# The first half of each expert's gate and up weights as one 4 MB transfer with 32 KB to a partition, in place of two of 2 MB with 16 KB

## The chip, the cores and the metric

One Trainium2 chip, one of its cores. The metric is the time on the device in microseconds (us), for the program from start to end, of one execution. Several executions of the same kernel are timed and the median is given.

## What is computed

The reference is one layer of a decoder block: 512 tokens of width 1024, in float32. An RMS norm and one input projection feed two attention branches (sliding window with sinks, and forgetting attention), whose gated outputs are added to x. Then comes the part that this document is about, a mixture of 32 experts with the top 4 for each token:

```python
logits = t @ w_router + b_router                       # t: the tokens after the second RMS norm
top_val, top_idx = lax.top_k(logits, 4); gate = softmax(top_val)
...
gu = xb @ w_gate_up[e] + b_gate_up[e]                  # w_gate_up[e]: 1024 x 2048, 8 MB
g, u = gu[:, :1024], gu[:, 1024:]
g = minimum(g, 7.0); u = clip(u, -7.0, 7.0)
a = (u + 1.0) * (g * sigmoid(1.702 * g))
return a @ w_down[e] + b_down[e]                       # w_down[e]: 1024 x 1024, 4 MB
```

The results are weighted with the gates and added to x. All 32 experts' weights, 12 MB each, are read once or more from HBM.

## The kernel before, in words

The first 420 us are the attention part. It streams w_in, w_o and w_out through two staging buffers (loop over `g`, lines 511 to 527), and its end frees the memory that the experts' weights go into.

Then the experts are worked off one at a time. The work on one expert is an item i; items are ordered so that even ones have room for 96 tokens (three groups of 32) and odd ones for 64 (two groups). Item 0 is done ahead of the loop, a loop over `pair` does items 1 and 2, 3 and 4, and so on (15 pairs here), and item 31 comes last (lines 1921 to 1969). An expert with more tokens than its room gets further items; the trace here has 32.

**Weights.** The 8 MB of gate and up weights of an item have one place in SBUF: six of the eight chunks of 128 rows in `gu_head`, two in `gu_tail`. They are loaded in four transfers of 2 MB (`load_gu`, line 546), q = 0 to 3. Each brings 256 neighbouring rows of the matrix, two neighbouring rows to a partition, so 16 KB in one piece to each partition (`w_gu_v`, line 349). So chunk k of an item does not hold the rows 128k to 128k + 127, but every second row of a block of 256 (`every_second`, line 441), and the tokens' values have to be laid out in the same order. The 4 MB of down weights come in two transfers of 2 MB (`load_dn`), with four rows to a partition, and have two places, `dn_even` and `dn_odd0/1`.

**Transfers.** SyncE (SP) issues all weight transfers in one queue, in the order of its program (lines 590 to 598): for item i the four of gate and up, then the two of down. Ahead of each it waits until TensorE has used what is in the place: `gu_used[q]` for q = 0, 1, 2, which TensorE raises after step k = 1, 3, 5 of `gate_up`, `bank_done` for q = 3, raised at step 7, and `dn_used[j]` for the down weights. The loads for item i + 1 are thus issued while item i runs.

**TensorE.** In `gate_up` (line 1843) it goes through the eight chunks k, for each group of tokens and each of four column blocks one matmul (line 1853). At even k it waits for the transfer that brings chunks k and k + 1 (`gu_in[k // 2]`). In even items of the loop it adds in between, after k = 1, 3, 5 and 6, the sums that bring the results of earlier items back to their tokens (`pair_sums`, line 1819). After `gate_up(i)` come a few small matmuls for the next list of tokens (line 1799) and `down(i - 1)` (lines 1888 and 1896).

**Tokens.** POOL fetches the rows of the item's tokens from HBM with an indirect DMA (`xg`, line 693, on a queue of its own). VectorE turns them in blocks of 32x32 into `xT` (even items) or `xT_odd` (`turn_rows`, line 1284): for each group and each quarter of 32 partitions one transpose of 32x256, with the columns picked two neighbours to a partition (line 1295), then a multiplication with the norm's gains, `g2_near`, laid out in the same order (loaded at line 543). For item 0 TensorE picks the rows itself by matmuls with a selection matrix (`first_rows`, line 1804), whose stationary operand is read with a step of 2 (line 1809).

Of the kernel before, what the change touches and what calls it, by code (L numbers as in the profile page):

```python
# [28 lines left out]
P = 128  # L29
# [27 lines left out]
def hybrid_block(nc, x, positions, norm1_g, w_in, b_forget, b_gate, q_norm_swa, k_norm_swa, sinks,  # L57
# [41 lines left out]
    with ExitStack() as ctx:  # L99
# [230 lines left out]
        ps = ctx.enter_context(nc.psum_tensor("ps", [P, 8, 512], F32))  # L330
        SUM_STEPS = (1, 3, 5, 6)
        SUM_BANKS = slice(6, 8)
        LAST_BANKS = (slice(0, 2), slice(2, 4), slice(6, 8), slice(4, 6))
# [14 lines left out]
        w_out_v = w_out[0].rearrange("(k p) n -> p k n", p=P)  # L348
        w_gu_v = w_gate_up.rearrange("l e (q p a) n -> (l e) q p (a n)", p=P, a=2)
        w_dn_v = w_down.rearrange("l e (j p k) n -> (l e) j p (k n)", p=P, k=4)  # L350

# [7 lines left out]
        b_dn_in = sem("b_dn_in")  # L359
        gu_in = [sem(f"gu_in{q}") for q in range(KD // 2)]  # L360
        dn_in = [[sem(f"dn_in{a}{j}") for j in (0, 1)] for a in (0, 1)]
# [41 lines left out]
        xT_ps, xT_ready = sem("xT_ps"), sem("xT_ready")  # L403
        gu_used = [sem(f"gu_used{q}") for q in range(KD // 2)]
        bank_done, gu_out, gu_biased = sem("bank_done"), sem("gu_out"), sem("gu_biased")
# [34 lines left out]

        def every_second(t):
            return slice(t // 2 * 2 * P + t % 2, (t // 2 + 1) * 2 * P, 2)

# [62 lines left out]
        def _(sp):  # L506
# [4 lines left out]
            for g in range(G_END):  # L511
                if g >= 2:
                    sp.wait_ge(split_lo, g - 1)
                dst, s = st_w[:, g % 2], stage_in[g % 2]
                if g < 2 * N_WIDE:
                    c0 = g // 2 * 2 * GW
                    sp.dma_start(st_w_wide[g % 2], w_in_v[:, g % 2 * KH:(g % 2 + 1) * KH, c0:c0 + 2 * GW]).then_inc(s, 16)
                elif g < G_O:
                    c0 = g * GW if g < G_GATE else GATE + (g - G_GATE) * GW
                    sp.dma_start(dst, w_in_v[:, :, c0:c0 + GW]).then_inc(s, 16)  # L520
                elif g < G_OUT:
                    c0 = (g - G_O) * GW
                    sp.dma_start(dst[:, 0:4], w_oa_v[:, :, c0:c0 + GW]).then_inc(s, 16)
                    sp.dma_start(dst[:, 4:8], w_ob_v[:, :, c0:c0 + GW]).then_inc(s, 16)
                else:
                    c0 = (g - G_OUT) * GW
                    sp.dma_start(dst, w_out_v[:, :, c0:c0 + GW]).then_inc(s, 16)
                if g == 0:
                    sp.dma_start(wfl[:, :, 0:HF], w_in_v[:, :, FL:FL + HF]).then_inc(wfl_in, 16)
                if g == 1:  # L530
                    sp.dma_start(bf_bc[:, :], b_forget[0].partition_broadcast(P)).then_inc(small_in, 16)
                    sp.dma_start(sink_bc[:, :], sinks[0].partition_broadcast(P)).then_inc(small_in, 16)
                    sp.dma_start(brt[:, :], b_router[0].partition_broadcast(P)).then_inc(small_in, 16)
                    sp.dma_start(g_sw[:, 0, :], q_norm_swa[0].partition_broadcast(P)).then_inc(small_in, 16)
                    sp.dma_start(g_sw[:, 1, :], k_norm_swa[0].partition_broadcast(P)).then_inc(small_in, 16)
                    sp.dma_start(w_rt[:, :, :], w_router[0].rearrange("(k p) e -> p k e", p=P)).then_inc(small_in, 16)
                    with nc.allow_non_contiguous_dma(reason="a few hundred words onto partitions"):
                        sp.dma_start(pos_i[:, :], positions[0].rearrange("(c p) -> p c", p=P)).then_inc(small_in, 16)
                        for a, w in enumerate((q_norm_fox, k_norm_fox)):
                            for half in (0, 1):  # L540
                                sp.dma_start(g_fx[half * HD:(half + 1) * HD, a:a + 1],
                                             w[0].rearrange("(d o) -> d o", o=1)).then_inc(small_in, 16)
                        sp.dma_start(g2_near[:, :].rearrange("p (q a) -> p q a", a=2),
                                     norm2_g[0].rearrange("(q p a) -> p q a", p=P, a=2)).then_inc(small_in, 16)

            def load_gu(e, q):
                src = w_gu_v[e, q] if isinstance(e, int) else w_gu_v[bass.ds(e, 1), q].rearrange("a p n -> (a p) n")
                two = gu_head[:, 2 * q:2 * q + 2, :] if q < 3 else gu_tail[:, :, :]
                sp.dma_start(two.rearrange("p a n -> p (a n)"), src).then_inc(gu_in[q], 16)

# [5 lines left out]
            sp.wait_ge(m_sum, KD)  # L556
            for q in range(3):
                load_gu(0, q)
# [4 lines left out]
            sp.wait_ge(split_lo, G_END)  # L563
            load_gu(0, 3)

# [12 lines left out]
            def gu_free(q, i, pair=None):  # L578

                if q < KD // 2 - 1:  # L580
                    sp.wait_ge(gu_used[q], counted(2, i, pair))
                else:
                    sp.wait_ge(bank_done, counted(5, groups_before(i), pair))

            for q in range(KD // 2):
                gu_free(q, 1)
                load_gu(e1, q)
            sp.wait_ge(items_ready, 1)
            n_pairs = sp.value_load(pairs[0:1, 0:1], min_val=PAIRS, max_val=MAX_PAIRS)
            with sp.Fori(0, n_pairs) as pair:  # L590
                for i in (2, 3):
                    e = sp.value_load(experts[0:1, bass.ds(pair * 2 + i, 1)], min_val=0, max_val=E - 1)
                    for q in range(KD // 2):
                        gu_free(q, i, pair)
# [346 lines left out]
        def _(dve):  # L941
# [57 lines left out]
            v.memset(ekey_col[0:1, :], 65536.0)  # L999
            dve.wait_ge(small_in, 16 * 12)  # L1000
            then(v.tensor_copy(pos_f[:, :], pos_i[:, :]))
# [282 lines left out]
            def turn_rows(i, pair=None):  # L1284
# [3 lines left out]
                if i > 1:  # L1288
                    dve.wait_ge(bank_done, counted(5, groups_before(i - 1), pair))
                near = xg[:, :].rearrange("s (k p a) -> s p k a", p=P, a=2)  # L1290
                for n in range(groups(i)):
                    s = slice(n * GROUP, (n + 1) * GROUP)
                    for q in range(4):
                        r = slice(q * GROUP, (q + 1) * GROUP)
                        ins = v.transpose(turned_rows[r, :, s].rearrange("r (k a) s -> r k a s", a=2),  # L1295
                                          near[s, r].rearrange("s p k a -> s k a p"))
# [181 lines left out]
        def _(pe):  # L1478
# [323 lines left out]
            def first_rows(ks):  # L1802
# [3 lines left out]
                for k in ks:  # L1806
                    dst = xT_a[:, k, :] if k < 5 else xT_b[:, k - 5, :]
                    for c in range(NB):
                        ins = pe.matmul(dst, h2n[:, c, every_second(k)], sel_f[:, c, :], start=(c == 0), stop=(c == NB - 1))
                return ins  # L1810
# [32 lines left out]
            def gate_up(i, pair=None, last=False):  # L1843
# [4 lines left out]
                for k in range(KD):  # L1848
                    if k % 2 == 0:
                        pe.wait_ge(gu_in[k // 2], counted(32, i * 16 + 16, pair))  # L1850
                    for n in range(groups(i)):
# [3 lines left out]
                        if k == KD - 1:  # L1855
                            ins.then_inc(bank_done, 1)
                    if k % 2 and k < KD - 1:
                        ins.then_inc(gu_used[k // 2], 1)
                    if i == 2 and k in SUM_STEPS:
# [133 lines left out]
```

## Time and profile before

| | us |
|---|---|
| Median of 3 runs | 1430.1 |
| Lowest and highest | 1428.09 and 1431.43 |
| The profiled execution's own time | 1430.49 |
| Its span in the profile | 1428.7 |
| TensorE busy with matmuls | 1367.9 (96%) |
| VectorE busy | 747.2 (52%) |
| DMA | 447.28 MB, 313 GB/s in the mean over the span |

The profile is that of one execution. The span goes from the first to the last recorded instruction; the time on the device holds 1.8 us more. A busy TensorE in this table includes matmuls that overlap in its pipeline. The times in the rows below count from the start of the span. A transfer's "time to landing" goes from its issue on SP to the arrival of the last part of its data and so includes the wait behind the transfers that are still in the queue.

### The profile page before, as it was taken

Reading aid. Unit: us, or ns where it says so; the run is one execution under the profiler, and the core shown is the slowest. Engines: PE = TensorE matmul, PEld = TensorE weight load, DVE = VectorE, ACT = ScalarE, POOL = GpSimd, SP = SyncE. Lnnn points to the kernel's source line nnn. Section 1 sums busy time; section 2 is a strip of 40 time slices with the busy share of each in tenths; the row PEclk is TensorE's granted clock in tenths of the full one; section 3 lists DMA queues with packets and bytes.
Section 4 is the critical chain, followed back from the end, with each engine's and each line's share of the span. In section 5 each row is a group of like instructions: output and inputs, shape, how many; then the busy total and the mean of one; then the engine's idle time right before and its main releaser. Section 6 shows DMA issues by size and latency. Waiting matters only on the chain.

```text
span 1428.7 us, 27526 instructions
## 1 busy us (share of the span) xinstructions
PE 1367.9 (96%) x11224; PEld 648.9 (45%) x11227; DVE 747.2 (52%) x1486; ACT 223.1 (16%) x416; POOL 190.5 (13%) x242
## 2 busy tenths in 40 slices
PE   6999999999989999999999999999999999999998
PEld 5888887778953333323232322323232232323233
DVE  5213736755257475545645544564654446465544
ACT  4224436642220000000000000000000000000000
POOL 2001400000002112020211202021120202112020
PEclk9999999999999999999999999999999999999999
DMA  6232320003679999999999999999999999999993
GB/s 192 89 118 64 113 89 1 2 31 114 255 295 356 409 400 417 391 412 414 413 413 405 417 403 407 417 409 414 411 416 393 414 417 409 412 414 415 395 414 154
DMA packets 59704, 447.28 MB, mean 313 GB/s; under 512 B 8656, under 2 KB 26096, under 8 KB 35056
## 3 DMA queue, kind: packets, MB, share of 16 engines
q1 hardware_dynamic: 56480, 435.96, 76.5%
q0 software_dynamic: 3072, 10.49, 2.3%
q8 instruction: 28, 0.46, 0.1%
q10 hardware_dynamic: 112, 0.28, 0.1%
q14 instruction: 12, 0.10, 0.0%
HBM read 442.51 MB, written 4.19 MB: 313 GB/s over the span
## 4 chain that ended last, share of the span: by engine, by line
PE 74%; DMA 19%; issue 4%; DVE 2%; ACT 1%; POOL 0%; SPq 0%; DVEq 0%; POOLq 0%; ACTq 0%
PE ps L1853 31%; DMA gu_head<-in_w_gate_up_dram 10%; PE ps L1888 9%; DMA gu_tail<-in_w_gate_up_dram 9%; PE ps L1819 7%; PE ps L1512 3%; PE ps L1514 3%; PE ps L1513 3%; PE ps L1896 2%; PE ps L1536 2%; PE ps L1538 2%; PE ps L1537 2%; PE ps L1503 1%; PE ps L1505 1%; PE ps L1504 1%
## 5 line engine op out<-in xcount | busy, mean ns | idle before, releaser
L1853 PE MATMUL ps<-gu_head,xT 128*32 128x512 f32 x2304 | 257.1, 594 | 2.5 <-DMA gu_head<-in_w_gate_up_dram 2.4
L1343 DVE TENSOR_TENSOR x_tok<-x_tok,ps 128x1024 f32<-128x1024 f32 x64 | 77.9, 1220 | 249.4 <-PE ps L1819 249.4
L1853 PE MATMUL ps<-gu_head,xT_odd 128*32 128x512 f32 x1536 | 168.9, 593 | 0.7 <-DVE act_gu L1307 0.6
L914 ACT ACTIVATE act_s<-act_gu 128x768 f32<-128x768 f32 (+1 forms) x32 | 23.6, 738 | 925.3 <-DVE act_gu L1318 925.3
L1853 PEld LDWEIGHTS ps<-gu_head,xT 128*32 128x32 f32 x2304 | 70.8, 110 | 168.7 <-issue 158.0
L1307 DVE STREAM_TRANSPOSE act_gu<-ps 128x512 f32<-128x512 f32 x80 | 57.2, 715 | 142.1 <-PE ps L1853 137.1
L693 POOL DMA_INDIRECT xg<-h_dram,idx_g x32 | 69.9, 2186 | 441.8 <-DVE row_all L1276 441.8
L954 DVE TENSOR_TENSOR st_l<-st_w,st_h 128x2048 fp32r<-128x2048 f32 x25 | 57.3, 2292 | 113.7 <-ACT st_h L758 113.7
L1888 PE MATMUL ps<-dn_even,aT 128*32 128x512 f32 x1024 | 116.1, 594 | 0.0
L1888 PE MATMUL ps<-dn_odd,aT 128*32 128x512 f32 x960 | 106.1, 594 | 0.0
L1853 PEld LDWEIGHTS ps<-gu_head,xT_odd 128*32 128x32 f32 x1536 | 49.3, 110 | 116.5 <-issue 111.3
L1853 PE MATMUL ps<-gu_tail,xT_odd 128*32 128x512 f32 x512 | 68.1, 680 | 28.2 <-DMA gu_tail<-in_w_gate_up_dram 28.2
L1853 PE MATMUL ps<-gu_tail,xT 128*32 128x512 f32 x768 | 88.8, 596 | 0.0
L1295 DVE STREAM_TRANSPOSE xT<-xg 32x256 f32<-32x256 f32 x180 | 77.8, 432 | 2.3
L1888 PEld LDWEIGHTS ps<-dn_even,aT 128*32 128x32 f32 x1024 | 31.7, 110 | 68.0 <-issue 67.6
L1896 PE MATMUL ps<-dn_even,aT 128*32 128x512 f32 x512 | 60.8, 592 | 0.0
L1888 PEld LDWEIGHTS ps<-dn_odd,aT 128*32 128x32 f32 x960 | 29.7, 110 | 63.2 <-issue 62.8
L1295 DVE STREAM_TRANSPOSE xT_odd<-xg 32x256 f32<-32x256 f32 x128 | 55.2, 431 | 1.8 <-DMA xg<-h_dram,idx_g 0.2
L721 POOL COPY put_row<-row_all 128x1 f32 x15 | 2.8, 185 | 382.9 <-PE ps L1819 382.9
L1853 PEld LDWEIGHTS ps<-gu_tail,xT_odd 128*32 128x32 f32 x512 | 17.4, 122 | 77.8 <-DMA gu_tail<-in_w_gate_up_dram 39.4
L758 ACT CAST st_h<-st_w 128x2048 fp32r<-128x2048 f32 x25 | 47.6, 1905 | 32.1 <-PE ps L1538 30.1
L1512 PE MATMUL ps<-hT_h,st_h 128*128 128x512 f32 x128 | 50.0, 391 | 0.0
(389 smaller groups left out, 2030.8 us busy)
## 6 DMA issues: line engine op xcount, KB each, us to landing
gu_head<-in_w_gate_up_dram SPq DMA_DIRECT2D x96, 2048.0 KB, 23.7
gu_tail<-in_w_gate_up_dram SPq DMA_DIRECT2D x32, 2048.0 KB
dn_even<-in_w_down_dram SPq DMA_DIRECT2D x32, 2048.0 KB, 25.1
dn_odd<-in_w_down_dram SPq DMA_DIRECT2D x32, 2048.0 KB, 21.4
st_w<-in_w_in_dram SPq DMA_DIRECT2D x17, 1024.0 KB, 5.3
st_w<-in_w_out_dram SPq DMA_DIRECT2D x4, 1024.0 KB, 5.1
x_tok<-in_x_dram SPq DMA_DIRECT2D x4, 512.0 KB, 5.7
st_w<-in_w_o_swa_dram SPq DMA_DIRECT2D x4, 512.0 KB, 3.5
```

Source lines behind the costliest of these rows:

```text
L693: g.indirect_dma_start(out=xg[0:n, :], out_offset=None, in_=h2_dram[:, :], in_offset=bass.IndirectOffsetOnAxis(ap=idx_g[0:n, 0:1], axis=0) ...
L758: sc.copy(st_h[:, g % 2], st_w[:, g % 2]).then_inc(split_hi, 1)
L954: v.tensor_tensor(st_l[:, g % 2], st_w[:, g % 2], st_h[:, g % 2].bitcast(F32), ALU.subtract).then_inc(split_lo, 1)
L1295: ins = v.transpose(turned_rows[r, :, s].rearrange("r (k a) s -> r k a s", a=2), near[s, r].rearrange("s p k a -> s k a p"))
L1307: ins = v.transpose(act_gu[:, :, n * GROUP:(n + 1) * GROUP].rearrange("p (b k) s -> p b k s", k=4), ps[:, n, :].rearrange("p (b r k) -> p ...
L1343: v.tensor_tensor(x_tok[:, c, :].rearrange("p (h n) -> p h n", h=2), x_tok[:, c, :].rearrange("p (h n) -> p h n", h=2), ps[:, banks, :], A ...
L1512: pe.matmul(dst, wh[:, k], xh[:, k], start=(k == 0), stop=False)
L1513: pe.matmul(dst, wh[:, k], xl[:, k], start=False, stop=False)
L1819: ins = pe.matmul(ps[:, banks, :][:, h], table[rows, c * P:(c + 1) * P], half[rows, :], start=(at == 0 and half is y_hi[y]), stop=(at == l ...
L1853: ins = pe.matmul(ps[j * GROUP:(j + 1) * GROUP, n, :], rows_of(i)[:, k, n * GROUP:(n + 1) * GROUP], gu_columns(k, j), start=(k == 0), stop ...
L1888: ins = pe.matmul(ps[u * GROUP:(u + 1) * GROUP, 5, :], aT[:, 4 * j + k, u % 2 * GROUP:(u % 2 + 1) * GROUP], dn_chunk(i, j)[:, k * D + u // ...
L1896: ins = pe.matmul(ps[u * GROUP:(u + 1) * GROUP, 4, :], aT[:, 4 * j + ku, 2 * GROUP:], dn_chunk(i, j)[:, ku * D + u // 2 * 512:ku * D + (u ...
```

## The change

The four transfers of gate and up weights become three: the first brings 512 neighbouring rows, 4 MB, with four neighbouring rows (32 KB) to a partition, the other two are as before. `GU_CHUNKS` says which chunks each one fills. TensorE waits for the first at k = 0 and releases its place after k = 3. As chunks 0 to 3 now hold every fourth row of a block of 512, the tokens' values are laid out in that order: `turn_rows` does two transposes where it did one, one for the first four chunks (four neighbours to a partition) and one for the other four, `first_rows` reads with a step of 4 for k below 4, and `g2_near` is loaded in two DMAs.

```diff
+        GU_CHUNKS = (slice(0, 4), slice(4, 6), slice(6, 8))
...
+        w_gu_four = w_gate_up.rearrange("l e (q p a) n -> (l e) q p (a n)", p=P, a=4)
...
-        gu_in = [sem(f"gu_in{q}") for q in range(KD // 2)]
+        gu_in = [sem(f"gu_in{q}") for q in range(len(GU_CHUNKS))]
...
-        def every_second(t):
-            return slice(t // 2 * 2 * P + t % 2, (t // 2 + 1) * 2 * P, 2)
+        def rows_at(t):
+            return slice(t, 4 * P, 4) if t < 4 else slice(t // 2 * 2 * P + t % 2, (t // 2 + 1) * 2 * P, 2)
...
-                        sp.dma_start(g2_near[:, :].rearrange("p (q a) -> p q a", a=2),
-                                     norm2_g[0].rearrange("(q p a) -> p q a", p=P, a=2)).then_inc(small_in, 16)
+                        sp.dma_start(g2_near[:, 0:4], norm2_g[0, 0:4 * P].rearrange("(p a) -> p a", a=4)).then_inc(small_in, 16)
+                        sp.dma_start(g2_near[:, 4:KD].rearrange("p (q a) -> p q a", a=2),
+                                     norm2_g[0, 4 * P:].rearrange("(q p a) -> p q a", p=P, a=2)).then_inc(small_in, 16)
 
             def load_gu(e, q):
-                src = w_gu_v[e, q] if isinstance(e, int) else w_gu_v[bass.ds(e, 1), q].rearrange("a p n -> (a p) n")
-                two = gu_head[:, 2 * q:2 * q + 2, :] if q < 3 else gu_tail[:, :, :]
-                sp.dma_start(two.rearrange("p a n -> p (a n)"), src).then_inc(gu_in[q], 16)
+                view, at = (w_gu_four, 0) if q == 0 else (w_gu_v, q + 1)
+                src = view[e, at] if isinstance(e, int) else view[bass.ds(e, 1), at].rearrange("a p n -> (a p) n")
+                rows = gu_head[:, GU_CHUNKS[q], :] if q < 2 else gu_tail[:, :, :]
+                sp.dma_start(rows.rearrange("p a n -> p (a n)"), src).then_inc(gu_in[q], 16)
...
             sp.wait_ge(m_sum, KD)
-            for q in range(3):
+            for q in range(2):
                 load_gu(0, q)
...
-                if q < KD // 2 - 1:
+                if q < len(GU_CHUNKS) - 1:
                     sp.wait_ge(gu_used[q], counted(2, i, pair))
...
-                near = xg[:, :].rearrange("s (k p a) -> s p k a", p=P, a=2)
+                near_four = xg[:, 0:4 * P].rearrange("s (p a) -> s p a", a=4)
+                near = xg[:, 4 * P:].rearrange("s (k p a) -> s p k a", p=P, a=2)
                 for n in range(groups(i)):
                     s = slice(n * GROUP, (n + 1) * GROUP)
                     for q in range(4):
                         r = slice(q * GROUP, (q + 1) * GROUP)
-                        ins = v.transpose(turned_rows[r, :, s].rearrange("r (k a) s -> r k a s", a=2),
+                        v.transpose(turned_rows[r, 0:4, s], near_four[s, r].rearrange("s p a -> s a p"))
+                        ins = v.transpose(turned_rows[r, 4:KD, s].rearrange("r (k a) s -> r k a s", a=2),
                                           near[s, r].rearrange("s p k a -> s k a p"))
...
-                        ins = pe.matmul(dst, h2n[:, c, every_second(k)], sel_f[:, c, :], start=(c == 0), stop=(c == NB - 1))
+                        ins = pe.matmul(dst, h2n[:, c, rows_at(k)], sel_f[:, c, :], start=(c == 0), stop=(c == NB - 1))
...
-                    if k % 2 == 0:
-                        pe.wait_ge(gu_in[k // 2], counted(32, i * 16 + 16, pair))
+                    q = next(q for q, ks in enumerate(GU_CHUNKS) if k < ks.stop)
+                    if k == GU_CHUNKS[q].start:
+                        pe.wait_ge(gu_in[q], counted(32, i * 16 + 16, pair))
...
-                    if k % 2 and k < KD - 1:
-                        ins.then_inc(gu_used[k // 2], 1)
+                    if k == GU_CHUNKS[q].stop - 1 and k < KD - 1:
+                        ins.then_inc(gu_used[q], 1)
```

## Rows read from the trace of the kernel before

**Rows 1.** Page, part 2: span in 40 slices, busy tenths and GB/s.

```profile
PE   6999999999989999999999999999999999999998
...
GB/s 192 89 118 64 113 89 1 2 31 114 255 295 356 409 400 417 391 412 414 413 413 405 417 403 407 417 409 414 411 416 393 414 417 409 412 414 415 395 414 154
```

**Rows 2.** Chain of waits, whole span: start us, length us, what.

```profile
506.89 13.73 PE ps L1853 x128
...
566.07 13.73 PE ps L1853 x128
...
1322.59 23.16 DMA gu_head<-in_w_gate_up_dram
1345.80 5.36 PE ps L1853 x48
1351.16 1.59 PE ps L1819 x12
```

**Rows 3.** Windows: two pairs late in the loop, three short ones.

```profile
core 0: us, PE busy (x) PEld busy (x) DVE busy (x) ACT busy (x) POOL busy (x), PEclk, DMA share, GB/s
1219.98:1345.80 125.82, 120.77 (x1081) 39.15 (x1081) 66.88 (x135) 6.61 (x11) 19.00 (x14) 0.99 1.01 411
480.00:485.00 5.00, 5.00 (x48) 1.88 (x42) 0.08 (x1) 0.00 (x0) 0.00 (x0) 1.00 1.03 439
485.00:490.00 5.00, 5.00 (x50) 1.60 (x52) 1.22 (x1) 0.00 (x0) 0.00 (x0) 1.00 1.00 423
510.00:515.00 5.00, 5.00 (x52) 1.56 (x48) 2.93 (x8) 0.00 (x0) 0.00 (x0) 1.00 1.01 340
```

**Rows 4.** Timeline of SP around each issue: start us, length us, engine, line.

```profile
17.79 0.81 SPq L543 DMA_DIRECT2D g_near<-in_norm_g_dram  x1
...
428.08 0.33 SPq L549 DMA_DIRECT2D gu_head<-in_w_gate_up_dram  x1
...
434.37 0.34 SPq L549 DMA_DIRECT2D gu_head<-in_w_gate_up_dram  x1
...
454.78 0.33 SPq L549 DMA_DIRECT2D gu_head<-in_w_gate_up_dram  x1
...
1326.02 0.33 SPq L549 DMA_DIRECT2D gu_head<-in_w_gate_up_dram  x1
```

**Rows 5.** DMA, us to landing, issued in 440:441, 454:456, 1320:1324, 1324:1328.

```profile
gu_head<-in_w_gate_up_dram SPq DMA_DIRECT2D x1, 2048.0 KB, 7.6
...
gu_head<-in_w_gate_up_dram SPq DMA_DIRECT2D x1, 2048.0 KB, 12.9
...
gu_head<-in_w_gate_up_dram SPq DMA_DIRECT2D x1, 2048.0 KB, 23.2
...
gu_head<-in_w_gate_up_dram SPq DMA_DIRECT2D x1, 2048.0 KB, 26.5
```

**Rows 6.** Page, part 3: DMA queue, packets, MB, share of 16 engines.

```profile
q1 hardware_dynamic: 56480, 435.96, 76.5%
q0 software_dynamic: 3072, 10.49, 2.3%
```

**Rows 7.** TensorE after idleness: timeline, and a window (columns as in rows 3).

```profile
701.12 3.64 PE L1853 MATMUL ps<-gu_tail,xT_odd 128*32 128x512 f32 x32 [1.85 <-DMA gu_tail<-in_w_gate_up_dram]
...
763.81 5.34 PE L1853 MATMUL ps<-gu_tail,xT_odd 128*32 128x512 f32 x32 [2.53 <-DMA gu_tail<-in_w_gate_up_dram]
...
765.00:766.00 1.00, 1.00 (x12) 0.31 (x8) 0.00 (x0) 0.00 (x0) 0.00 (x0) 0.50 1.08 459
```

**Rows 8.** Timelines of POOL, VectorE and TensorE around an even item's rows.

```profile
506.00 2.45 POOL L693 DMA_INDIRECT xg<-h_dram,idx_g  x1 [3.72 <-DVE row_all L1276]
...
521.33 5.33 DVE L1295 STREAM_TRANSPOSE xT<-xg 32x256 f32<-32x256 f32 x12
526.70 0.96 DVE L1299 TENSOR_TENSOR xT<-xT,g_near 128x768 f32<-128x768 f32 x1
...
531.07 2.33 PE L1853 MATMUL ps<-gu_head,xT 128*32 128x512 f32 x20
```

**Rows 9.** DMA issues of the whole span: the row gathers, median us to landing.

```profile
xg<-h_dram,idx_g POOLq DMA_INDIRECT x32, 10.8
```

More of the change, by code:

```diff
@@ L403, in hybrid_block @@
         xT_ps, xT_ready = sem("xT_ps"), sem("xT_ready")
-        gu_used = [sem(f"gu_used{q}") for q in range(KD // 2)]
+        gu_used = [sem(f"gu_used{q}") for q in range(len(GU_CHUNKS))]
         bank_done, gu_out, gu_biased = sem("bank_done"), sem("gu_out"), sem("gu_biased")
@@ L563, in _ @@
             sp.wait_ge(split_lo, G_END)
-            load_gu(0, 3)
+            load_gu(0, 2)
             sp.wait_ge(group_done, G_END)
@@ L583, in gu_free @@
                     sp.wait_ge(bank_done, counted(5, groups_before(i), pair))
-            for q in range(KD // 2):
+            for q in range(len(GU_CHUNKS)):
                 gu_free(q, 1)
@@ L592, in _ @@
                     e = sp.value_load(experts[0:1, bass.ds(pair * 2 + i, 1)], min_val=0, max_val=E - 1)
-                    for q in range(KD // 2):
+                    for q in range(len(GU_CHUNKS)):
                         gu_free(q, i, pair)
@@ L999, in _ @@
             v.memset(ekey_col[0:1, :], 65536.0)
-            dve.wait_ge(small_in, 16 * 12)
+            dve.wait_ge(small_in, 16 * 13)
             then(v.tensor_copy(pos_f[:, :], pos_i[:, :]))
```

## The prediction

> **What bounds the kernel now.** I read the page's slices first [rows 1]: TensorE is near full in nearly every slice, but in most slices from the fourteenth on the core also moves 400 GB/s or more. Two resources are full at once, so the chain of waits has to say which one sets the end [rows 2]. Call the work on one expert an item, and an odd item with the even one behind it a pair. Early on, a pair is TensorE's alone: the same piece comes at 506.89 and at 566.07, 59.2 us apart, and no transfer stands between them in the chain. Later nearly every pair has a DMA piece of 20 us or more in it, the time from the issue of a weight transfer to its landing. The last is that of the first quarter of item 30's gate and up weights, issued at 1322.59; TensorE starts the item at 1345.80, and no weight transfer follows in the chain: the 82.9 us from there to the end of the span are TensorE's and the last sums'.
>
> The stretches say how full the DMA is [rows 3]. Two pairs late in the loop take 125.82 us with a DMA share of 1.01; that is 62.9 us a pair, 3.7 more than TensorE needs, and 24 transfers of 2 MB: 5.24 us each. In windows without a gather the rate is 423 to 439 GB/s (431 in the mean), so 2 MB (2.097 million bytes) take 4.8 to 5.0 us, say 4.9. What 24 x 4.9 = 117.6 us leave of 125.8 belongs to the four row gathers of the stretch, 2.05 us each; a window with one runs at 340 GB/s. The end is therefore set by three things: when the DMA stream begins to run without gaps, how many bytes it has to bring before item 30 can start, and its rate.
>
> **The change, part by part.** *The wait at the head of an item.* TensorE now waits for 4 MB where it waited for 2. At item 30 the first quarter lands at 1345.8 (1322.59 + 23.2), the second at 1352.5 (1326.02 + 26.5) [rows 4, 5]: 6.7 us later, a transfer and most of a gather beside it. The even item's start is the DMA-bound point, and all behind it is TensorE's, so this is **+6.7 us**, paid once: in the loop only the phase between the two shifts, the period stays the DMA's.
>
> *The release of the buffer.* The first 4 MB of item i+1 can be issued only after step k = 3 of item i instead of half of it after k = 1. With a full queue this costs nothing. Count from the start of an even item, with four transfers outstanding (two of gate/up, two of down, to about +21 us): step 3 is done at +12.4 (two blocks of 5.4 and a sum of 1.6 [rows 2]), and 8.6 us of work still lie before the new transfer. From the odd item's start at +35 (59.2 less the odd item's own 24.2, 506.89 to 531.07 [rows 2, 8]) step 3 is done at +42, and the queue holds ten transfers' work, to +52. This backlog is the cover; if it were gone, each issue would lose the two steps of waiting, 7 us.
>
> The one place without backlog is the beginning. There the transfers of item 1 are issued as item 0 frees its quarters, the first two at 428.08 and 434.37 [rows 4], 6.3 us apart where one takes 4.9: there are gaps. Now the first 4 MB go out at 434.37. A 2 MB transfer on a nearly empty queue lands after 7.6 us [rows 5], so these land at 434.37 + 7.6 + 4.9 = 446.9, about when TensorE is done with item 0 (a wait of a few us would stay in its slack); the other two at 456.7, the gather of item 2 adds 2.05, and the 4 MB of item 2 land at 468.6. Before, the second of these quarters landed at 454.78 + 12.9 = 467.7. The stream is **+0.9 us** late: the old one lost nearly as much by its gaps as the new one by its late start. The ends are nothing and 6.3 us, the whole distance of the first two issues.
>
> *The rate.* A 2 MB transfer is 128 rows of 16 KB, eight on each of 16 engines; if a 32 KB row goes as one packet, each engine has eight packets fewer in an item, 248 in the 31 items of the stream. No row shows such a packet. From above: queue 1 has 56,480 packets, 435.96 MB and 76.5% of 16 engines' time [rows 6], 17,488 us; at the best window's 439 GB/s the bytes alone take 15,890, so at most 28 ns go to each packet: a gain of 7.0 us. From below: if long rows run as in the slowest of the gapless windows (423 against 431), 31 x 9.8 us get 1.9% longer, 5.8 us. Between them I take **-2.0 us**, nearer to nothing, because the windows with 16 KB packets alone already run at the highest rates here. The Trainium skill (DMA: Bandwidth & Descriptors, Where 436 GB/s comes from) puts the ceiling at 435.2 GB/s; if all that 431 lacks to it were paid per packet, the estimate by that page would be a gain of 1 to 2 us. The trace's windows lie on both sides of that figure.
>
> *TensorE's clock.* After 1.85 us of idleness 32 matmuls take 3.64 us; after 2.53 us they take 5.34, with the granted clock at 0.50, the 1.2 GHz level [rows 7]. In the new loop the whole slack, 3.7 us, falls ahead of even items. A dip there costs 1.7 us, hidden in the slack (3.7 becomes 2.0) except at item 30, where it goes to the end. Since a dip shortens the next idleness, I take half: **+0.9 us**, ends 0 and 1.7.
>
> *Costed at nothing.* The turning of rows on VectorE: 12 transposes of 32x256, 5.33 us in all, become 24 of 32x128. If each half cost as much as a whole, xT, ready at 527.7 (526.70 + 0.96), would be ready at 533.0, 1.9 us after TensorE's 531.07 [rows 8]; the 3.7 us ahead of even items cover it, and the 3.6 us of an odd item's eight too. The gather goes through POOL's own queue but shares the engines with long rows. It is issued at 506.00 and its rows are turned from 521.33 on; the median landing takes 10.8 us [rows 8, 9], and doubled it would be 6 us late, which the slack of 3.4 and 3.7 us covers. SP issues two DMAs for the norm2 gains instead of one, which took 0.81 us [rows 4], so the third w_in load starts that much later; TensorE is then busy with the first two loads, and if it weren't, this would be the price. In each item SP has one wait and one issue fewer; behind its longer wait for k = 3 stand only loads whose buffers come free later still. The first rows' matmuls read h2n with step 4 instead of 2, and their number stays.
>
> The sum: 6.7 + 0.9 - 2.0 + 0.9 = **+6.5 us**. The profiled execution took 1430.49 us (span 1428.7), 0.4 over the median of 1430.1; so 1437.0 for it and **1436.6** as a median.
>
> **The rivals.** *A cost per transfer goes (faster).* As a mechanism of this kernel: with the queue full, a transfer takes 5.24 us with gathers, and at the best rate 4.78, so at most 0.46 us can be a cost per transfer. 31 transfers fewer give -14.3, with +8.5 for the rest -5.8 us: 1424.3. It decides from 0.27 us a transfer upwards. Against it: the spread of the gapless windows leaves only 0.1 to 0.2. The same sign would come if long packets softened the gathers, which cost 2.05 us where their bytes (10.49 MB / 32) need 0.8 [rows 6]. Together 0.14. The Trainium skill (DMA: Bandwidth & Descriptors, Anatomy of one DMA) gives each DMA 2.0 us beside its bytes and advises large ones; taken in full that would be 62 us for 31 transfers, and in a full queue the trace does not agree, as the 5.24 us show.
>
> *It cancels (no change).* The gain per packet at its upper end and no clock dip: 6.7 + 0.9 - 7.0 = +0.6, so 1430.7. Chance 0.17.
>
> *The queue runs dry.* If the late issue at the beginning costs its full 6.3, with a dip and no gain, it is 6.7 + 6.3 + 1.7 = +14.7: 1444.8; 5.8 more if long rows run slower. 0.09.
>
> *It doesn't do what it says:* each row goes as two packets of 16 KB. Then the gain of 2.0 is missing, +8.5, 1438.6. This is inside the forecast.
>
> **How the numbers follow.** The forecast with its own range (+3 to +11) has 0.60. The range of 8 in 10 goes from just below no change, 1429.0, to 1445.0, the bound of the dry queue. A measurement of this kernel can tell some 0.2%, 2.9 us. Slower by more: 0.60 + 0.09, 0.69; within: 0.17; faster: 0.14.
>
> **What the profile after would show.** The chain should hold gu_head pieces ahead of even items and few or none of gu_tail, and TensorE's waits for gu_tail should go over to gu_head. Item 30 should start 5 to 8 us after 1345.8, and the last 83 us be the same but for a clock dip. The DMA should be near idle until about 435 us and full from then on, two late pairs should take 125 us, and the packet count fall by 32 x 128 = 4,096 if rows go whole. The prediction is wrong if two pairs take under 124 us (a gain in rate), if the DMA's share falls inside the loop (a dry queue), or if even items wait for VectorE.

## The result, and the profile after

| | before | after |
|---|---|---|
| Median, us | 1430.76 (4 runs) | 1440.8 (4 runs) |
| Lowest to highest | 1428.09 to 1431.5 | 1439.46 to 1444.72 |
| Profiled execution: time, span | 1430.49, 1428.7 | 1444.72, 1442.9 |
| Ratio, with its 95% interval | | 1.0082 (1.0065 to 1.0099) |

The change makes the kernel slower by 0.82%, 11.7 us (9.3 to 14.2). The ratio is formed from the single executions and is not the quotient of the two medians, which lie 10.0 us apart; here and below, a difference in us is the ratio's share of the time before, unless it is read from a profile. The forecast was slower by 6.5 us: the right side, and little more than half of the size. The time of 1440.8 us lies inside the range of 8 in 10 (1429.0 to 1445.0); the 11.7 us lie just above the forecast's own range of +3 to +11. The profiled execution of after is the slowest of its four, 14.2 us over the profiled one of before.

First the page of after, the lines that answer to [rows 1] and [rows 6]: TensorE in 40 slices, GB/s, packets.

```profile
PE   6999999999999999999999999998998999899998
...
GB/s 190 90 115 81 95 88 2 2 59 155 199 274 344 397 394 414 397 416 413 413 409 410 414 401 413 415 410 412 411 414 394 413 410 412 409 408 415 397 415 80
DMA packets 54984, 447.28 MB, mean 310 GB/s; under 512 B 8032, under 2 KB 25472, under 8 KB 34432
## 3 DMA queue, kind: packets, MB, share of 16 engines
q1 hardware_dynamic: 51760, 435.96, 75.5%
```

The eleventh slice from the left onwards shows the later start of the stream (199, 274, 344 GB/s for 255, 295, 356). The packets fell by 4,720, and 624 of these are small, under 512 B (8,656 became 8,032). The other 4,096 are the long rows, which go as one packet each where two went. Of the small ones 512 are 16 for each of the 32 transfers saved (the kernel of rows alone below shows this: 512 small packets with its first 32 transfers, 256 with the next 16), and 112 belong to the norm2 gains. In the loop the rate is what it was.

The chain of waits near its end, to be held against [rows 2].

```profile
708.98 19.33 DMA gu_head<-in_w_gate_up_dram
...
1276.56 19.49 DMA gu_head<-in_w_gate_up_dram
1296.09 5.36 PE ps L1860 x48
...
1338.19 20.55 DMA gu_head<-in_w_gate_up_dram
1358.79 7.05 PE ps L1860 x48
```

Item 30 starts at 1358.79 for 1345.80: 13.0 us later. Its first block takes 7.05 us for 5.36, the clock dip that the forecast had at half price. The rest to the end of the span is 84.1 us for 82.9. Behind item 1 all DMA pieces of the chain are now gu_head ahead of even items, and TensorE's waits moved as forecast, from gu_tail (the line of before first) to gu_head:

```profile
PE ps L1853 <- DMA gu_tail<-in_w_gate_up_dram: 28.2, 12, 3.2
...
PE ps L1860 <- DMA gu_head<-in_w_gate_up_dram: 38.0, 14, 3.9
```

Two late pairs, to be held against the first stretch of [rows 3] (same columns):

```profile
1106.26:1232.77 126.51, 120.46 (x1081) 39.38 (x1081) 73.92 (x175) 6.41 (x10) 18.98 (x14) 0.99 1.01 409
1232.77:1358.79 126.02, 120.47 (x1080) 39.34 (x1081) 72.99 (x174) 6.41 (x10) 19.00 (x14) 0.99 1.01 409
```

The period is the DMA's, 126.0 and 126.5 us for 125.8: the queue is full, nothing was gained, and little lost. Over the last ten pairs the same holds. The chain of before has this piece ten pairs ahead of item 30:

```profile
692.61 23.15 DMA gu_head<-in_w_gate_up_dram
```

It landed at 715.76, and item 30's first quarter at 1345.75, 630.0 us later. In after the first half of the same item landed at 728.31 (708.98 + 19.33) and item 30's at 1358.74, 630.4 us later. So 12.6 of the 13 us are there ten pairs before the end: they lie at the beginning or in the phase, and the longer rows gained nothing in these pairs. What the forecast did not have stands at the head of the expert part. These are item 0's selection matmuls, first in before, then in after (timelines of TensorE).

```profile
410.70 1.15 PE L1809 MATMUL ps<-sel_f,h2n 128*128 128x96 f32 x8 [0.37 <-ACT sel_f L905]
412.43 8.26 PE L1809 MATMUL ps<-sel_f,h2n 128*128 128x96 f32 x56
```

```profile
408.93 2.08 PE L1815 MATMUL ps<-sel_f,h2n 128*128 128x96 f32 x8 [0.37 <-ACT sel_f L909]
411.58 12.56 PE L1815 MATMUL ps<-sel_f,h2n 128*128 128x96 f32 x56
```

The 64 records are those of 32 matmuls (eight chunks, four blocks of tokens), of which the 16 with k below 4 read with step 4. They take 14.6 us instead of 9.4, on the path: item 0 can't start without them, and item 1's transfers wait for item 0. Everything ahead of them ran 1.8 us earlier in this execution.

### The profile page after: what moved, and what is told of

It reads as the page before. It is cut to its first block, busy times and chain, and to the rows that moved or that the text cites. A ratio compares the mean times of both kernels' runs of the same rounds, so it can differ in the third digit from the quotient of the medians.

```text
span 1442.9 us, 27744 instructions
## 1 busy us (share of the span) xinstructions
PE 1374.8 (95%) x11227; PEld 653.9 (45%) x11227; DVE 798.7 (55%) x1794; ACT 221.7 (15%) x416; POOL 189.1 (13%) x242
## 2 busy tenths in 40 slices
DMA packets 54984, 447.28 MB, mean 310 GB/s; under 512 B 8032, under 2 KB 25472, under 8 KB 34432
## 4 chain that ended last, share of the span: by engine, by line
PE 72%; DMA 21%; issue 4%; DVE 1%; ACT 1%; POOL 0%; SPq 0%; DVEq 0%; POOLq 0%; ACTq 0%
PE ps L1860 32%; DMA gu_head<-in_w_gate_up_dram 19%; PE ps L1895 8%; PE ps L1825 7%; PE ps L1518 3%; PE ps L1520 3%; PE ps L1519 3%; PE ps L1542 2%; PE ps L1543 2%; PE ps L1544 2%; PE ps L1509 1%; PE ps L1510 1%; PE ps L1511 1%; PE ps L1815 1%; DMA gu_tail<-in_w_gate_up_dram 1%
## 5 line engine op out<-in xcount | busy, mean ns | idle before, releaser
L1860 PE MATMUL ps<-gu_head,xT 128*32 128x512 f32 x2304 | 268.8, 616 | 38.0 <-DMA gu_head<-in_w_gate_up_dram 38.0
L1300 DVE STREAM_TRANSPOSE xT<-xg 32x128 f32<-32x128 f32 x180 | 73.8, 410 | 2.3
L1860 PE MATMUL ps<-gu_tail,xT_odd 128*32 128x512 f32 x512 | 59.6, 607 | 2.3 <-DMA gu_tail<-in_w_gate_up_dram 2.3
L1300 DVE STREAM_TRANSPOSE xT_odd<-xg 32x128 f32<-32x128 f32 x128 | 52.2, 408 | 1.6
L1542 PE MATMUL ps<-st_h,hT_h 128*128 128x512 f32 x128 | 49.9, 390 | 0.0
```

The source lines that it names most:

```text
L1300: v.transpose(turned_rows[r, 0:4, s], near_four[s, r].rearrange("s p a -> s a p"))
L1542: pe.matmul(dst, hT_h[:, k0 + k, rows], st_h_wide[half][:, k], start=(half == 0 and k == 0), stop=False)
L1860: ins = pe.matmul(ps[j * GROUP:(j + 1) * GROUP, n, :], rows_of(i)[:, k, n * GROUP:(n + 1) * GROUP], gu_columns(k, j), start=(k == 0), stop ...
```

## The experiments

The theory after seeing this (A): the excess is the reading with step 4, and the terms of the forecast hold. Rivals: the long rows, VectorE's transposes, or the late release. All ratios are to executions of the kernel before that were taken beside each run; 0.1% is 1.43 us. Where the medians give a clearly other difference, the text says so.

**The step alone.** The kernel before with

```diff
-    ins = pe.matmul(dst, h2n[:, c, every_second(k)], sel_f[:, c, :], ...
+    ins = pe.matmul(dst, h2n[:, c, (every_fourth(k) if k < 4 else every_second(k))], sel_f[:, c, :], ...
```

> The kernel before, with the first rows' matmuls reading h2n with a step of 4 for k below 4 (item 0's tokens are then laid out in an order that its weights do not have). Theory A: the excess of the change over the forecast is these 64 matmuls; their weight loads are slower with step 4, item 0 starts 4 to 5 us later, every later transfer with it, and the time is 4 to 5 us over before: about 1435.5. Rival B: the excess is the DMA's (long rows) or VectorE's, and these matmuls were slow in the run of after only because the granted clock happened to be 0.50 there: then this run is within 1 us of before, 1430.8.

Measured: 1435.02 for 1430.64, ratio 1.0035 (1.0023 to 1.0047), 5.0 us (3.3 to 6.7). Theory A holds. Its timeline:

```profile
410.17 2.15 PE L1809 MATMUL ps<-sel_f,h2n 128*128 128x96 f32 x8 [0.37 <-ACT sel_f L905]
413.28 12.47 PE L1809 MATMUL ps<-sel_f,h2n 128*128 128x96 f32 x56
```

**The change without the step.** The changed kernel with `rows_at` as the old `every_second`.

> The changed kernel, with the first rows' matmuls reading with a step of 2 throughout (the same effect on item 0's order of rows). Theory A: 4 to 5 us faster than the changed kernel, about 1436, that is the forecast's 6 us over before; item 0's gate_up starts as early as before. Rival B: as slow as the changed kernel, 1440.8.

Measured: 1437.17, ratio 1.0059 (1.0044 to 1.0074), 8.4 us over before. The matmuls are fast again:

```profile
410.52 1.15 PE L1815 MATMUL ps<-sel_f,h2n 128*128 128x96 f32 x8 [0.37 <-ACT sel_f L909]
412.25 6.73 PE L1815 MATMUL ps<-sel_f,h2n 128*128 128x96 f32 x56
```

But 8.4 is more than the 6.5 of the forecast, so another term may be too small. It is no more than a hint: the interval is 6.3 to 10.6 us, the six executions spread from 1432.56 to 1441.87, and the medians lie 6.5 us apart.

How long these matmuls take varies from one execution to the next, and all fourteen profiles, of the two kernels and of the twelve runs that compute the layer, show it at this place. With step 2 they take 9.4 us in five profiles and 7.9 in three (8.26 or 6.73 for the 56 records, 1.15 for the eight ahead); with step 4 they take 14.6 in two and 13.1 to 13.3 in four. The means, 8.8 and 13.7, are 4.8 us apart, which agrees with the 5.0 of the run.

The next four runs split the 4 MB transfer in the changed kernel's layout.

**Two transfers, each waited for and released alone.**

```diff
-        GU_CHUNKS = (slice(0, 4), slice(4, 6), slice(6, 8))
+        GU_CHUNKS = (slice(0, 2), slice(2, 4), slice(4, 6), slice(6, 8))
...
-                view, at = (w_gu_four, 0) if q == 0 else (w_gu_v, q + 1)
+                view, at = (w_gu_four, 0) if q < 2 else (w_gu_v, q)
                 src = ...
+                if q < 2:
+                    src = src[:, q * 2 * F2:(q + 1) * 2 * F2]
```

> The changed kernel's layout (four neighbouring rows to a partition), but the first half again in two transfers, each of two of the four rows (16 KB pieces), each waited for and released on its own. Theory A: the head wait and the late release go (7 to 8 us), the step 4 stays: 4 to 5 us over before, 1435. Rival B (the layout costs nothing, all is in the 4 MB transfer): 1430.8. If VectorE's longer transposes mattered, it would stay above 1436.

Measured: 1433.71, ratio 1.0022 (1.0011 to 1.0033), 3.2 us (1.6 to 4.7). Less than the 4 to 5 expected, but clear of zero: with head wait and late release gone, what is left fits the size of the step, whose interval it overlaps.

**Two transfers, both issued after k = 3, both waited for at k = 0.** On top of the run before:

```diff
-                    sp.wait_ge(gu_used[q], counted(2, i, pair))
+                    sp.wait_ge(gu_used[max(q, 1)], counted(2, i, pair))
...
-                    if k == GU_CHUNKS[q].start:
+                    if k == GU_CHUNKS[q].start and q != 1:
                         pe.wait_ge(gu_in[q], counted(32, i * 16 + 16, pair))
+                    if k == 0:
+                        pe.wait_ge(gu_in[1], counted(32, i * 16 + 16, pair))
```

> As the run before it, but both transfers are issued after k = 3 and both waited for at k = 0: the changed kernel in all but the size of the pieces, 16 KB instead of 32. Theory A: the size of a row does nothing: 1440.8 within 1.5 us, two late pairs in 125.8 to 126.5 us. Rival C (long rows cost rate): 2 to 5 us faster than the changed kernel. Rival D (long rows gain rate): 2 us slower.

Measured: 1442.91, ratio 1.0090 (1.0077 to 1.0103), 12.9 us. The changed kernel's cost is all there with 16 KB pieces. It may be 1 us or so slower than with 32 KB, which these intervals do not resolve.

**One of the two at a time.** First only the waits of the diff above (both at k = 0), each transfer released alone:

> The layout of the changed kernel, the first half in two transfers of 16 KB pieces, each released after its own two steps (k = 1, k = 3), but both waited for at k = 0. The step 4 of the first rows stays, worth 5.0 us over before. Theory A: the head wait alone adds 6 to 7 us, and the late release little (0.9 as forecast): 1430.6 + 5.0 + 6.7 + clock 0.9 = 1443, the same as with the late release (1442.9) within 1.5 us. Rival E (the late release, by the gaps in the queue, is what costs): 1436.

Measured: 1439.01 for 1429.87, ratio 1.0068 (1.0048 to 1.0088), 9.7 us. Then only the late release:

> As the run before it, the other way round: each transfer waited for alone, both released (and issued) after k = 3. Theory A: no head wait, so only the step 4 and the late start of the stream: 1430.6 + 5.0 + 0.9 = 1436.5, within 1.5 us. Rival E: 1443.

Measured: 1435.61, ratio 1.0046 (1.0028 to 1.0064), 6.6 us. The first number was expected too high and both leave the same reading. The four kernels form a square, in us over before:

| | released alone | released late |
|---|---|---|
| waited for alone | 3.2 | 6.6 |
| both waited for at k = 0 | 9.7 | 12.9 |

The head wait costs 6.5 and 6.3, the late release 3.4 and 3.2, each with some 3 either way, so the two values for the late release are each hardly clear of zero. Theory A and rival E had each put the excess on one of the two alone; by these numbers both cost. The late release then would be several times the 0.9 of the forecast, which the square by itself does not show. Where would it be paid?

**The late release, at the beginning and in the loop.** The kernel before, with `gu_free(max(q, 1), 1)` for item 1 alone:

> The kernel before; only item 1's first transfer is issued late, after k = 3 of item 0 instead of k = 1. Theory A: the late release costs at the beginning, where the queue has gaps, and that shift of the stream stays to the end: the 3.3 us by which the late release made the split kernels slower, 2.5 to 4 us over before, 1433. Rival (it costs in the loop, where the queue is full, or nowhere): 1430.

and with `gu_free(max(q, 1), i, pair)` in the loop alone:

> The kernel before; the first transfer is issued late (after k = 3) for the items from 2 on, in the loop, and item 1's as before. Theory A: the backlog of 8 us and more covers it: 1430, within 1 us. Rival: 3 us more.

Measured: 1434.79 for 1430.08, ratio 1.0025 (1.0012 to 1.0038), 3.6 us for one single transfer issued late; and 1430.91, ratio 1.0008 (0.9997 to 1.0019), 1.1 us and not clear of zero, for thirty of them. The 3.6 us have an interval of 1.7 to 5.4, so this run is clear of the 0.9. The cover in the loop is real; the price is paid once, where the stream begins. The windows there show why it was under-sized, first in before, then in this run (columns as in [rows 3]):

```profile
430.00:440.00 10.00, 10.00 (x90) 3.19 (x86) 6.40 (x21) 0.00 (x0) 0.83 (x1) 1.00 0.98 362
440.00:450.00 10.00, 9.36 (x92) 2.88 (x92) 7.34 (x17) 0.00 (x0) 1.79 (x3) 1.00 0.92 334
```

```profile
430.00:440.00 10.00, 10.00 (x94) 3.26 (x90) 6.00 (x20) 0.00 (x0) 1.16 (x1) 1.00 0.49 153
440.00:450.00 10.00, 9.36 (x92) 2.74 (x88) 7.02 (x18) 0.00 (x0) 1.17 (x2) 1.00 1.00 429
```

The prediction took the two issues 6.3 us apart for gaps. But the DMA of before was busy for 98% and 92% of these stretches: from 430 to 440 us queue 1 alone took 87% and 89% of the two halves, and item 1's own gather, issued at 429.67 on the other queue, another 4% and 15%. With the late issue 5.1 us of the 20 are empty instead of 1.0; item 0 started 0.6 us later in this execution, and about 3.5 us remain.

**The head wait, in odd and in even items.** The kernel before, with both transfers waited for at k = 0 in odd items, then in even ones:

> The kernel before; odd items wait at k = 0 for both of the first two transfers, even ones as before. Theory A: the start of an odd item is not bound by its transfers (they land 3 us and more ahead): 1430 within 1 us. Rival (any head wait costs): 3 us or more.

> The kernel before; even items wait at k = 0 for both of the first two transfers, odd ones as before. Theory A: the whole of the head wait is here, 6.4 us (5 to 7.5): 1436.5. Rival (it costs by the count of waits, half in even and half in odd items): 1433.

Measured: even 1437.61, ratio 1.0045 (1.0031 to 1.0059), 6.4 us, as expected. Odd 1433.24, ratio 1.0021 (1.0010 to 1.0031), 3.0 us: a miss, nothing was expected. Its chain shows a second DMA piece behind item 30's:

```profile
1321.85 22.87 DMA gu_head<-in_w_gate_up_dram
...
1344.76 5.36 PE ps L1855 x48
...
1357.20 23.45 DMA gu_head<-in_w_gate_up_dram
...
1380.79 7.07 PE ps L1855 x64
```

With even items starting as early as before, item 31's second transfer has not landed when TensorE comes to it: the start lies 36.0 us behind item 30's instead of 35.0. After the last even item nothing absorbs that. That is 1 us of the 3; where the rest comes from stays open, since this execution (1430.7, near the fastest of its kernel) does not show it. In the changed kernel the even item itself starts later and this wait does not arise.

**The change turned round.** The kernel before with the first four chunks in transfers of 1 MB, `GU_CHUNKS = (slice(0, 1), slice(1, 2), slice(2, 3), slice(3, 4), slice(4, 6), slice(6, 8))`, in the old layout:

> The kernel before with the change turned round: the first four chunks in four transfers of 1 MB, each waited for and released alone. Theory A: the last even item can start when 1 MB of it has landed instead of 2, 2.4 us earlier, and TensorE then needs the next chunk every 2.7 us where the queue brings one every 2.45 (2.6 with gathers); with small losses at later chunks 1.5 to 2.4 us faster than before: 1428.7. If half as long pieces (8 KB) cost rate, up to 4.5 us of it are given back: no change or 2 us slower. Rival (the phase between the queue and TensorE doesn't set the end): 1430.6.

Measured: 1434.46 for 1429.87, ratio 1.0037 (1.0024 to 1.0051), 5.3 us slower: a miss. The chain shows a bound that a finer head does not move:

```profile
1312.57 21.41 DMA gu_tail<-in_w_gate_up_dram
1334.02 5.34 PE ps L1859 x32
...
1349.98 5.15 PE ps L1859 x48
```

The start of an even item has a second bound, the last transfer of the odd item ahead of it and TensorE's 16 us behind that, and in the chain of before the two bounds take turns from pair to pair, so they lie close together. A finer head moves only the first bound, and the smaller pieces and a clock dip (5.34 for 3.64) come on top. What share each of these has was not tried.

**VectorE alone.** The kernel before with the changed `turn_rows`:

> The kernel before with the changed kernel's turning of rows on VectorE (24 transposes of 32x128 for 12 of 32x256 in an even item, half of them reading with step 4; the tokens of items from 1 on are then in an order that their weights do not have). All theories but one: VectorE's 2.6 us more in an even item are hidden, 1430.6 within 1 us. The one (VectorE delays TensorE at the head of even items): 1 us a pair where TensorE is the bound, up to 2 us in all.

Measured: 1429.32, ratio 1.0000 (0.9988 to 1.0012). Hidden, as forecast.

**Rows and steps by themselves.** A kernel without the layer. SyncE's core, a buffer being free when its last transfer has landed:

```python
N = 16
BUF = 4
...
for f, (form, per) in enumerate(((pairs, 2), (long_rows, 1), (halves, 2), (singles, 4), (long_rows, 1))):
    for n in range(N):
        if n >= BUF:
            sp.wait_ge(landed[f][n % BUF], 16 * per * (n // BUF))
        form(n, n % BUF, landed[f][n % BUF])
    ...
```

> A kernel of its own that computes nothing of the layer: SyncE streams 16 x 4 MB of w_gate_up in each of five stretches, drained between: as two transfers of 2 MB with 16 KB rows, as one of 4 MB with 32 KB rows, as two of 2 MB with 16 KB pieces of the 32 KB rows, as four of 1 MB with 8 KB pieces, and the 32 KB rows once more. Beside it TensorE does six groups of 48 matmuls of 128x128x96 whose weights are read with steps 1, 2, 4, 1, 4, 2, each after 12 large ones, and VectorE the transposes of 32x256 with step 2 and of 32x128 with step 4. Theory A (the gain of -2.0 us in the forecast is real, 16 ns for each packet saved): the 4 MB stretches are 1% faster than the 2 MB ones. Rival C: no difference, within 0.2%, or a loss. For the step: weights with step 4 take longer to load than with step 2 also where the granted clock is 1.00 (2.08 us instead of 1.15 for eight matmuls, as at the head of the first rows), steps 1 and 2 the same; the rival is that the clock alone is to blame.

Measured, in one execution, in the timeline of SP (first issue of each stretch) and in windows inside the stretches:

```profile
4.01 122.22 SPq L51 DMA_DIRECT2D buf<-in_w_gate_up_dram  x32
164.61 119.25 SPq L43 DMA_DIRECT2D buf<-in_w_gate_up_dram  x16
322.44 121.07 SPq L47 DMA_DIRECT2D buf<-in_w_gate_up_dram  x32
481.94 133.94 SPq L55 DMA_DIRECT2D buf<-in_w_gate_up_dram  x64
643.40 119.34 SPq L43 DMA_DIRECT2D buf<-in_w_gate_up_dram  x16
801.32 2.89 SPq L65 DMA_DIRECT2D out_dram<-xs  x4
```

```profile
168.00:318.00 150.00, 0.00 (x0) 0.00 (x0) 0.00 (x0) 0.00 (x0) 0.50 1.00 431
326.00:476.00 150.00, 0.00 (x0) 0.00 (x0) 0.00 (x0) 0.00 (x0) 0.50 1.01 429
486.00:636.00 150.00, 0.00 (x0) 0.00 (x0) 0.00 (x0) 0.00 (x0) 0.50 1.01 422
647.00:797.00 150.00, 0.00 (x0) 0.00 (x0) 0.00 (x0) 0.00 (x0) 0.50 1.00 433
```

From start to start, 64 MB take 160.6 us with 16 KB rows, 157.8 and 157.9 with 32 KB rows, 159.5 as 16 KB pieces of the long rows, and 161.5 as 8 KB pieces. The form with 32 KB rows gains 1.6 to 2.8 us in 64 MB. The kernel streams 31 x 4 MB of them, so by this 3.1 to 5.4 us: theory A, and more than the 2.0 of the forecast. (The 16 ns for each packet in the expectation are a slip: 2.0 us over 248 packets are 8 ns.) Two things stay open. The long rows also halve the number of transfers, so the gain may be the transfers': 16 fewer, 0.10 to 0.17 us each. And the stretch with 16 KB rows is the only one beside which TensorE and VectorE work, so the 1.6 us against the 16 KB pieces are the firmer figure. In the kernel itself the ten pairs above show no gain, where by this there should be 2.0 to 3.5 us. TensorE's timeline, for steps 1, 2 and 4, and windows at the head of and inside the stretch with step 4:

```profile
16.69 10.85 PE L92 MATMUL ps<-warm,xs 128*128 128x96 f32 x96
...
37.71 11.43 PE L92 MATMUL ps<-warm,xs 128*128 128x96 f32 x96
...
59.31 22.49 PE L92 MATMUL ps<-warm,xs 128*128 128x96 f32 x96
```

```profile
59.50:61.50 2.00, 2.00 (x11) 2.00 (x10) 0.00 (x0) 0.00 (x0) 1.00 1.02 434
...
63.50:65.50 2.00, 2.00 (x11) 2.00 (x10) 0.00 (x0) 0.00 (x0) 0.50 1.06 451
...
118.00:120.00 2.00, 2.00 (x10) 2.00 (x10) 0.00 (x0) 0.00 (x0) 0.50 1.06 451
```

Steps 1 and 2 cost nearly the same (0.113 and 0.119 us a record), step 4 twice as much, 0.234. With step 4 as many weight loads are done in 2 us at a granted clock of 1.00 as at 0.50. So the step alone makes these loads slow; and inside such a stretch, with TensorE always busy, the granted clock falls to 0.50, the 1.2 GHz level, both times that step 4 comes (the last line is from the second stretch, which begins at 113.96). The Trainium skill (SBUF — State Buffer, Door 1: The DMA port swizzle) says that SBUF is read in lines of 16 bytes and wants at least two accesses to a line for full speed; in float32, step 2 has two and step 4 one. The trace agrees with it in the times: 5% more at step 2, twice the time at step 4. That the lines are the reason no run here isolates.

In the kernel the slow loads are therefore only a part of the excess. Against the 7.9 us of the profiles with step 2 that kept the full clock, 14.6 is 6.8 us more. The 32 records with step 4 cost 3.7 of it (32 times 0.234 less 0.119). The rest, an estimate by difference, is the clock: in after it is granted at 0.51 in the last 6.9 us of these matmuls, where the records with step 2 run.

## Why the prediction was right or wrong

The forecast had the side, the bound and the place of the main term, and was too small. By its own steps:

- **The bound.** Right. The period stayed at 126 us for two pairs, the share of the DMA at 1.01, the chain's late pieces went from gu_tail to gu_head ahead of even items, and the change is paid once. But item 30 started 13.0 us later, where 5 to 8 had been named.
- **The wait at the head, +6.7.** Right: 6.4 (4.4 to 8.4) by the run with the wait in even items alone, 6.3 and 6.5 in the square. The medians of the first lie 7.5 us apart.
- **The late release, +0.9, with nothing in the loop.** The loop was right (1.1, not clear of zero). The beginning was under-sized: 3.6 measured (1.7 to 5.4). The 4 MB of item 2 landed at 458.24 + 15.3 = 473.5 in after; less the 3.45 us by which item 0 started later (425.56 for 422.11) that is 470.1, 2.4 us after the old 467.7 where 0.9 was worked out. The step that was mis-sized is "the old one lost nearly as much by its gaps as the new one by its late start": the DMA of before was busy for 98% and 92% in the windows from 430 to 450 us, with item 1's gather beside the first transfers, so it had lost little. In after the first and the third landing of item 1, at 450.6 and 463.8, are moreover 13.2 us apart for 11.85 by the forecast's prices; why is not shown.
- **The rate, -2.0.** Not settled. By the rows alone it is 3.1 to 5.4 us for 31 items, in one execution; in the kernel the period did not fall (630.4 us for 630.0 over ten pairs), and the changed kernel against the one with the same waits and 16 KB pieces (11.7 for 12.9 us) is within what the runs cannot tell.
- **TensorE's clock, +0.9.** Half the price fits what can be seen. Item 30's first block shows a dip in two of the five profiles in which an even item waits for its first four chunks at once: in after, 7.05 us, and in the run with the wait in even items, 6.72; in the other three it takes 5.36. The lines are of the run with the wait in even items and of the one with two transfers and one wait:

```profile
1352.78 6.72 PE ps L1855 x48
...
1355.49 5.36 PE ps L1864 x48
```

- **Costed at nothing.** For VectorE right. **For the first rows' matmuls wrong: this is the step that failed.** "Read h2n with step 4 instead of 2, and their number stays" counted instructions and took their time from the row of the old form. They took 14.6 us for 9.4, and the run with this alone is 5.0 us slower. It was not bounded from both sides as the other unknown costs were; twice the old time for the half of them that changes, +4.7 us, would have been the end of such a range, and with it the forecast's end at 1444.8 would have gone to 1449.5. Even that leaves out the clock, which with step 4 fell in the same place and took up the rest of the excess.

The measured terms add up within their margins: 6.4 + 3.6 + 5.0 = 15.0, with some 3 us either way and whatever clock dips came in these runs already in it. Less nothing to 5.4 for the rows it is 9.6 to 15.0; the change measured 11.7 (9.3 to 14.2). The changed kernel without the step measured 8.4 us (6.3 to 10.6) over before, so the failed step aside the forecast of 6.5 is at the low end, but not contradicted. Of the rivals, the queue that runs dry had the right place, the beginning, and some half of its price of 6.3. A cost per transfer of 0.10 to 0.17 us is not ruled out by the rows alone, which can't tell it from a cost per packet; it is under the 0.27 from which that rival decides. The row was not split: the packet count fell by the forecast's 4,096 beside the small ones.

## What to carry to other kernels

When a stream of weights is the bound, a larger transfer costs once at each end, as it did here: the consumer waits for more bytes at its last bound start (6.4 us), and the stream begins later where buffers come free piece by piece (3.6 us); in between a full queue hides it, so price the two ends and not the count of items. A layout that is free for the DMA can be dear for who reads it: an operand's step is a change of price even where no instruction is added, so check the readers of every tile whose order changes, those ahead of the loop too. And look for the second bound before making the first finer.

## What the hardware showed unexpectedly

- Weight loads of float32 (128x128) with a step of 4 elements take twice the time of steps 1 and 2 (0.234 for 0.113 and 0.119 us a record), at either level of the clock.
- In stretches of such loads the granted clock fell to 0.50 though TensorE was never idle, and the step-2 loads behind them ran at 0.51 too; with step 2 alone in the same place it was 1.00 in one execution and 0.79 on average in another (6.73 and 8.26 us for the same 56 records). Why the same matmuls differ so was not settled.
- VectorE's transposes feel the step too. A 32x128 block costs 0.41 us with step 4 in after, nearly the 0.43 of a 32x256 block with step 2:

```profile
L1300 DVE STREAM_TRANSPOSE xT<-xg 32x128 f32<-32x128 f32 x180 | 73.8, 410 | 2.3
L1301 DVE STREAM_TRANSPOSE xT<-xg 32x128 f32<-32x128 f32 x180 | 46.7, 260 | 0.0
```

- 64 MB in 16 transfers with 32 KB rows took 1.6 to 2.8 us less than in 32 transfers with 16 KB rows or pieces, though the gapless windows of before already ran at 423 to 439 GB/s. Each engine has 144 packets fewer, 16 of them small, which would be 11 to 19 ns a packet, if it is the packets; in the full kernel no such gain was seen.
